# Odd mixer of a hybrid decoder trunk: rotations before the fourth input block, index products and attention units one projection half earlier

## Chip, cores and metric
The kernel runs on one core of a Trainium2 chip. The metric is the device time of one execution in microseconds. The times given are medians of executions of the same program; the profile shows one further execution.

## What is computed
Two decoder layers over 256 tokens of width 1024, all in f32. The change lies in the mixer of the second, odd layer. Cut to that:

```python
def odd_layer(h, ...):
    proj = rms_norm(h, norm_mix) @ w_in                  # 1024 -> 2628 columns
    proj_c, proj_d = split(proj)                         # RWKV-7 | sparse attention
    y_c = rwkv7_time_mix(proj_c, ...)                    # token shift, low-rank gates, 8-head state
    q, k, v, qi, ki, wi = split_cols(proj_d)             # rotate q, k, qi, ki (partial_rope)
    y_d = dsa_attention(q, k, v, qi, ki, wi)
    h = h + concatenate([y_c, y_d]) @ w_out
    return h + moe_swiglu(rms_norm(h, norm_ffn), ...)    # top 2 of 8 experts

def rwkv7_time_mix(p, mu, ...):
    p = p + (prev - p) * mu                              # token shift
    r, k, v, wd, ad, gd = split_cols(p)
    decay, a = gates(tanh(wd) @ w_up), sigmoid(a0 + ad @ a_up)
    # k normalised per head, then a recurrence over the tokens

def dsa_attention(q, k, v, q_idx, k_idx, w_idx):
    score = sum_h relu(q_idx[h] @ k_idx.T) * w_idx[h]    # index products
    sel = top_k(causal(score), 64)
    return softmax(q @ k[sel].T * scale) @ v[sel]        # 8 heads, shared k and v
```

## The kernel before
Every engine has a list of instructions of its own, written out by hand, and works it off in order; semaphores tie the lists together. There is no scheduler: the order in the code is the order on the engine.

The input projection of the odd layer is cut into six blocks of 512 columns (the last narrower) and each block into two halves of the contraction, `odd_half(q, x)`. Blocks 0 to 2 are computed in three split products with `split_half`; blocks 3 to 5 in plain f32 with `whole_half`, 16 products of 128x256 per half. Blocks 0 to 2 bring, in the order of `ODD_PAIRS`, the low-rank inputs (pair 6) and all of the attention's parts (pairs 7 to 10, into `draw`); blocks 3 to 5 bring pairs 0 to 5, the r, k and v of the recurrence. Each pair is copied out of its bank by ScalarE (`odd_copy`, which counts `odd_copied`) and shifted in time by VectorE (`shift`, which counts `shifted`). A copy into the raw buffer waits until the shift but one before it is done.

TensorE puts other work between the halves. The rotations are products with a permutation (the three `C("perm")` matmuls, then the `dup` ones), followed by two pairs of transposes of values and index weights; VectorE finishes the rotation (`rope`). `index_products(t)` makes the index scores of token block t; ScalarE takes the relu (`relu_copy`), VectorE sums the heads (`index_scores`), picks the keys eight at a time (`select_keys`) and makes the mask (`key_mask`). Block 1's 8 rounds of selection are spread, two each, over the first four attention units.

Attention has `UNITS` = 8 units of two heads and one token block; units 0 to 3 are token block 0. It is a pipeline over u: in step u TensorE makes the scores of unit u, the value product of unit u-2 and the transposes of unit u-1, in this order; the transposes wait for `p_ready`. VectorE's `softmax(u)` first normalises unit u-1 (`p_ready`) and then masks the scores of unit u and takes their maximum; ScalarE's `odd_attention(u)` copies the output of unit u-2, takes the exponential of u and copies the transposed weights of u-1.

The RWKV preparation runs in the same loops: `rwkv_step(u - RWKV_LAG)` follows attention step u on VectorE and ScalarE. It needs the gates, which ScalarE makes after `low_rank`, and `low_rank` needs the last projection copy (`odd_copied` 11) and comes behind the last half. Its end is `tilde_done`, behind which the recurrence (the loop over t), the output projection and the experts follow.

Of the kernel before, what the change touches and what calls it, by code (L numbers as in the profile page):

```python
# [145 lines left out]
def trunk(nc, a, consts_dram, out):  # L146
# [297 lines left out]
    UNITS = KM * NT  # L444
# [5 lines left out]
    SCALE = HD ** -0.5  # L450
    RWKV_LAG = 2
    TWO_PI = 6.283185
# [150 lines left out]
    def _(act):  # L603
# [270 lines left out]
        for t in range(NT):  # L874
            act_.activation(Vd[:, t, :], bank[2][:, T * t + HD:T * t + 2 * HD], ACT.Copy)
            act_.activation(wi[:, t, :], bank[2][:, T * t + P + HD:T * t + P + HD + 4], ACT.Copy,
                            scale=4 ** -0.5 * HD ** -0.5).then_inc(sem("kv_copied"), 1)
        odd_copy(5)
        odd_copy(6)
        relu_copy(0)  # L880
        relu_copy(1)
        odd_copy(7)
        odd_copy(8)
        odd_attention(0)
        odd_attention(1)
        odd_copy(9)
        odd_copy(10)
# [29 lines left out]

        for u in range(2, UNITS + 2):
            odd_attention(u)
            rwkv_step(u - RWKV_LAG)  # L920
# [142 lines left out]
    def _(dve):  # L1063
# [381 lines left out]

        shift(0)
        shift(1)
        index_scores(0)
        select_keys(0, TOPK // 8)
        key_mask(0)  # L1450
        index_scores(1)
        shift(2)
        shift(3)

# [43 lines left out]
        for u in range(UNITS + 2):  # L1498
            softmax(u, UNITS, p0, lambda u: md[:, u // KM, :], None)
            if u == 1:  # L1500
                shift(4)
                shift(5)
            if u < KM:
# [335 lines left out]
    def _(pe):  # L1839
# [391 lines left out]
        for q in range(3):  # L2231
            for x in range(2):
                odd_half(q, x)
        pe.wait_ge(sem("odd_copied"), 2)
        odd_half(3, 0)
        pe.wait_ge(sem("odd_copied"), 5)
# [6 lines left out]
        for t in range(NT):  # L2243
            pe_.transpose(bank[2][:, T * t:T * t + P], draw[:, 4, t * P:t * P + P], ident)
            pe_.transpose(bank[2][:, T * t + P:T * t + P + HD + 4], draw[0:HD + 4, 7, t * P:t * P + P],
                          ident[0:HD + 4, 0:HD + 4]).then_inc(sem("kv_T"), 1)
        odd_half(3, 1)

# [26 lines left out]
        pe.wait_ge(sem("odd_rope"), 5)  # L2275
        index_products(0)
        pe.wait_ge(sem("kv_copied"), NT)
        pe.wait_ge(sem("odd_copied"), 4)
        odd_half(4, 0)
        index_products(1)  # L2280
        odd_half(4, 1)
        for u in range(UNITS + 2):
            attention(u, UNITS, lambda f, j: draw[HD * j:HD * j + HD, f, :],
                      lambda f, j: L1["kd"][HD * j:HD * j + HD, :],
                      lambda kt, h: Vd[:, kt, :], L1["pT"], dsa_first)
            if u < 2:
                if u == 0:
                    pe.wait_ge(sem("odd_copied"), 7)
                odd_half(5, u)
                if u:  # L2290
                    low_rank()
# [341 lines left out]
```

## Time and profile before

| | us |
|---|---|
| median of 3 timed runs | 1536.43 |
| lowest and highest | 1536.02, 1536.93 |
| profiled execution, its own time | 1535.13 |
| span of the profiled execution, first to last instruction | 1533.2 |
| TensorE (PE) busy | 1449.2 (95%) |
| VectorE (DVE) busy | 653.6 (43%) |
| ScalarE (ACT) busy | 258.8 (17%) |
| GpSimd (POOL) busy | 30.2 (2%) |
| mean granted clock of TensorE | 0.971 |

The odd mixer is in the page's span from about 385 to 583 us. Times in the trace count from the span's start. PE stands for TensorE, PEld for its weight loads, DVE for VectorE, ACT for ScalarE, SPq for SyncE's load queue. Each f32 product shows as two records, so a half of 16 products reads x32. What stands in brackets is the idle time of the engine ahead of a row and who ended it.

### The profile page before, as it was taken

The page shows a single profiled execution, that of the slowest core. Times are in us where ns is not written, and L with a number is a line of the kernel's source. Part 1 is how long each engine was busy: PE and PEld are TensorE (multiplying, and loading weights), DVE is VectorE, ACT ScalarE, POOL GpSimd, SP SyncE. Part 2 cuts the span into 40 slices and gives each one's busy share as a digit, 9 for nine tenths or more (in the row PEclk, how much of TensorE's full clock was granted, in tenths as well). Part 3 has the DMA queues.
Part 4 walks back from the last instruction along what each step waited for, and adds up shares of the span by engine and source line. Part 5 has one row for each costly group of instructions (what it writes and reads, how often), then busy time and mean ns, then how long its engine had stood idle before and what let it go on. Part 6 is the DMA issues. An engine that isn't in the chain of part 4 may idle for free.

```text
span 1533.2 us, 46200 instructions
## 1 busy us (share of the span) xinstructions
PE 1449.2 (95%) x21517; PEld 1384.2 (90%) x21517; DVE 653.6 (43%) x1549; ACT 258.8 (17%) x441; POOL 30.2 (2%) x33
## 2 busy tenths in 40 slices
PE   7898999998995889999999999999999999999997
PEld 6756899998883778999999999999999999999896
DVE  6942554445567662353334224234224323332327
ACT  2323453434325120200000000000000000000001
POOL 0000000000000210000000000000000000000000
PEclk9998999999995999999999999999999999999998
DMA  9040564445330007699999999999999999999994
GB/s 312 28 165 3 218 220 166 164 162 172 114 110 15 3 3 288 243 387 404 408 396 405 409 382 407 409 382 408 409 379 410 408 380 409 408 385 409 408 373 170
DMA packets 138183, 434.27 MB, mean 283 GB/s; under 512 B 10107, under 2 KB 13285, under 8 KB 137862
## 3 DMA queue, kind: packets, MB, share of 16 engines
q1 hardware_dynamic: 133536, 420.59, 71.2%
q10 hardware_dynamic: 2982, 5.45, 1.0%
q0 software_dynamic: 1472, 5.24, 1.0%
q8 instruction: 171, 2.80, 0.8%
q14 instruction: 22, 0.18, 0.0%
HBM read 426.42 MB, written 4.85 MB: 281 GB/s over the span
## 4 chain that ended last, share of the span: by engine, by line
PE 78%; DMA 9%; DVE 7%; ACT 3%; SPq 2%; issue 1%; ACTq 0%; DVEq 0%
PE bank L2540 31%; PE bank L2538 16%; PE bank L2147 4%; PE bank L2149 4%; PE bank L2148 4%; DMA ring<-in_moe_w_gate 4%; DMA ring<-in_moe_w_down 3%; PE bank L2217 3%; SPq L508 2%; PE bank L1889 2%; PE bank L2120 2%; DMA ring<-in_moe_w_up 2%; PE bank L2135 1%; PE bank L2055 1%; PE bank L2140 1%
## 5 line engine op out<-in xcount | busy, mean ns | idle before, releaser
L2538 PE MATMUL bank<-ring,yT 128*32 128x384 f32 x5760 | 634.4, 491 | 6.2 <-DMA ring<-in_moe_w_gate 5.0
L2540 PE MATMUL bank<-ring,yT 128*32 128x128 f32 x5760 | 635.5, 273 | 0.0
L2540 PEld LDWEIGHTS bank<-ring,yT 128*32 128x32 f32 x5760 | 629.2, 110 | 0.4
L2538 PE MATMUL bank<-ring,arena 128*32 128x384 f32 x2304 | 255.6, 490 | 0.9 <-DMA ring<-in_moe_w_down 0.9
L2540 PE MATMUL bank<-ring,arena 128*32 128x128 f32 x2304 | 255.8, 273 | 0.0
L2540 PEld LDWEIGHTS bank<-ring,arena 128*32 128x32 f32 x2304 | 251.4, 110 | 0.0
L1796 DVE TENSOR_TENSOR arena<-arena,bank 128x384 f32<-128x384 f32 x56 | 28.9, 551 | 426.6 <-PE bank L2540 284.4
L1744 DVE STREAM_TRANSPOSE arena<-arena 32x192 f32<-32x192 f32 x384 | 142.0, 370 | 114.0 <-PE bank L2540 108.9
L2149 PE MATMUL bank<-arena_r,ring_r 128*128 128x256 f32 x608 | 171.9, 283 | 0.0
L2538 PEld LDWEIGHTS bank<-ring,yT 128*32 128x32 f32 x5760 | 163.9, 108 | 7.7 <-issue 4.5
L2147 PE MATMUL bank<-arena_r,ring_r 128*128 128x256 f32 x528 | 148.0, 280 | 1.3 <-DVE arena_r L1324 1.3
L2148 PE MATMUL bank<-arena_r,ring_r 128*128 128x256 f32 x528 | 147.6, 280 | 0.0
L1039 ACT ACTIVATE arena<-bank 128x384 f32<-128x384 f32 x56 | 24.8, 488 | 681.8 <-PE bank L2540 681.8
L1311 DVE TENSOR_TENSOR ring_r<-ring,ring_r 128x2048 fp32r<-128x2048 f32 (+2 forms) x42 | 87.0, 2076 | 86.7 <-ACT ring_r L762 86.5
L2149 PEld LDWEIGHTS bank<-arena_r,ring_r 128*128 128x128 f32 x608 | 115.7, 190 | 0.0
L2147 PEld LDWEIGHTS bank<-arena_r,ring_r 128*128 128x128 f32 x528 | 99.5, 188 | 1.7 <-issue 1.4
L2148 PEld LDWEIGHTS bank<-arena_r,ring_r 128*128 128x128 f32 x528 | 99.1, 188 | 0.1
L762 ACT ACTIVATE ring_r<-ring 128x2048 fp32r<-128x2048 f32 (+2 forms) x42 | 72.9, 1741 | 91.2 <-PE bank L2149 86.4
L2538 PEld LDWEIGHTS bank<-ring,arena 128*32 128x32 f32 x2304 | 63.0, 108 | 1.5 <-DMA ring<-in_moe_w_down 1.5
L1889 PE MATMUL bank<-xnT,ring 128*128 128x256 f32 x192 | 46.8, 405 | 8.0 <-DVE arena L1281 5.7
L1889 PEld LDWEIGHTS bank<-xnT,ring 128*128 128x128 f32 x192 | 38.8, 205 | 15.0 <-DVE arena L1281 5.8
L2217 PE MATMUL bank<-xnT,ring 128*128 128x256 f32 x192 | 42.8, 381 | 0.0
(473 smaller groups left out, 1259.0 us busy)
## 6 DMA issues: line engine op xcount, KB each, us to landing
ring<-in_moe_w_gate SPq DMA_DIRECT2D x56, 2048.0 KB, 23.3
ring<-in_moe_w_up SPq DMA_DIRECT2D x56, 2048.0 KB, 23.3
ring<-in_moe_w_down SPq DMA_DIRECT2D x56, 2048.0 KB, 20.2
ring<-in_ffn_w_gate SPq DMA_DIRECT2D x5, 2048.0 KB, 7.9
ring<-in_ffn_w_up SPq DMA_DIRECT2D x5, 2048.0 KB, 7.8
ring<-in_ffn_w_down SPq DMA_DIRECT2D x5, 2048.0 KB, 7.6
ring<-in_o_w_in SPq DMA_DIRECT2D x5, 2048.0 KB, 7.9
ring<-in_e_w_in SPq DMA_DIRECT2D x4, 2048.0 KB, 16.9
```

The costliest lines, as they stand in the source:

```text
L508: sp.dma_start(w.rearrange("p (k n) -> p k n", k=src.shape[1]), src).then_inc(loaded, 16)
L762: act_.activation(pair(h, src.shape[1])[0], src, ACT.Copy).then_inc(sem("hi_done"), 1)
L1311: v.tensor_tensor(lo, src, hi.bitcast(f32), SUB).then_inc(sem("lo_done"), 1)
L1744: last = v.transpose(to[QUAD[b], :, 32 * a:32 * a + 32], Hc[QUAD[a], 0:to.shape[1], 32 * b:32 * b + 32])
L1889: last = pe_.matmul(dst(i)[0:width, :], w[:, k, i * P:i * P + width], xnT[:, k, :], start=(k == 0), stop=(k == KD - 1))
L2120: last = pe_.matmul(half(bank[2 + i // 2], i), view(n + i // 4)[:, k, (i % 4) * P:(i % 4) * P + P], yT[:, k, :], start=(k == 0), stop=(k = ...
L2147: pe_.matmul(dst, w[0], x[0], start=start, stop=False, skip_group_check=True)
L2148: pe_.matmul(dst, w[1], x[0], start=False, stop=False, skip_group_check=True)
L2149: return pe_.matmul(dst, w[0], x[1], start=False, stop=stop, skip_group_check=True)
L2217: last = pe_.matmul(half(b[i // 2], i), w[:, k, i * P:i * P + P], xnT[:, k, :], start=(k == 0 and i % 2 == 0), stop=(k == KD - 1), skip_gr ...
L2538: pe_.matmul(b[QUAD[m], 0:FM], x(m), w[:, 0:FM], start=start, stop=stop, skip_group_check=True)
L2540: last = pe_.matmul(b[QUAD[3], P * m:P * m + P], x(m), w[:, FM:FB], start=start and m == 0, stop=stop, skip_group_check=True)
```

## The change
No instruction is added or taken away. On TensorE the rotations, with the transposes behind them, move ahead of half (3,0); the index products and the attention steps 0, 1 and 2 each move ahead by one projection half, so that attention step 0 stands before half (4,1), step 1 before (5,0), and step 2 before (5,1), with `low_rank` behind that. On ScalarE the relu copies, and the attention steps 0 to 2, move ahead of copies accordingly. On VectorE the index scores and key selection of block 0 move ahead of shifts 0 and 1, shifts 2 and 3 move from ahead of `softmax(0)` to behind it, and 4 and 5 from behind `softmax(1)` to behind `softmax(2)`. `RWKV_LAG` grows from 2 to 3.

```diff
--- before.py
+++ after.py
@@ -448,7 +448,7 @@
         return (u // NT, u % NT) if base == 0 else (u % KM, u // KM)
 
     SCALE = HD ** -0.5
-    RWKV_LAG = 2
+    RWKV_LAG = 3
     TWO_PI = 6.283185
 
     block = ctx.enter_context(nc.Block())
@@ -875,14 +875,15 @@
             act_.activation(Vd[:, t, :], bank[2][:, T * t + HD:T * t + 2 * HD], ACT.Copy)
             act_.activation(wi[:, t, :], bank[2][:, T * t + P + HD:T * t + P + HD + 4], ACT.Copy,
                             scale=4 ** -0.5 * HD ** -0.5).then_inc(sem("kv_copied"), 1)
+        relu_copy(0)
         odd_copy(5)
         odd_copy(6)
-        relu_copy(0)
         relu_copy(1)
+        odd_attention(0)
         odd_copy(7)
         odd_copy(8)
-        odd_attention(0)
         odd_attention(1)
+        odd_attention(2)
         odd_copy(9)
         odd_copy(10)
 
@@ -915,7 +916,7 @@
                                 L1["st8"][:, 0:16][:, :, None].to_broadcast([P, 16, HD]), ACT.Copy).then_inc(
                     step("kk_wide")[0], 1)
 
-        for u in range(2, UNITS + 2):
+        for u in range(3, UNITS + 2):
             odd_attention(u)
             rwkv_step(u - RWKV_LAG)
         for u in range(UNITS + 2 - RWKV_LAG, UNITS + 2):
@@ -1443,14 +1444,12 @@
             link(v.tensor_scalar(work, work, -2.0e38, NEG, ALU.is_gt, MUL))
             link(v.tensor_tensor(md[:, t, 0:nk], work, C(f"causal{t}")[:, 0:nk], ADD))
 
-        shift(0)
-        shift(1)
         index_scores(0)
         select_keys(0, TOPK // 8)
         key_mask(0)
+        shift(0)
+        shift(1)
         index_scores(1)
-        shift(2)
-        shift(3)
 
         def rwkv_step(u):
 
@@ -1497,9 +1496,9 @@
 
         for u in range(UNITS + 2):
             softmax(u, UNITS, p0, lambda u: md[:, u // KM, :], None)
-            if u == 1:
-                shift(4)
-                shift(5)
+            if u in (0, 2):
+                shift(2 + u)
+                shift(3 + u)
             if u < KM:
                 select_keys(1, TOPK // 8 // KM)
                 if u == KM - 1:
@@ -2231,8 +2230,6 @@
         for q in range(3):
             for x in range(2):
                 odd_half(q, x)
-        pe.wait_ge(sem("odd_copied"), 2)
-        odd_half(3, 0)
         pe.wait_ge(sem("odd_copied"), 5)
         for i, x in enumerate((draw[:, 0:2, :], draw[:, 2:4, :], draw[:, 5:7, :])):
             pe_.matmul(bank[5 + i][:, :], C("perm"), flat(x), start=True, stop=True).then_inc(sem("odd_rope_P"), 1)
@@ -2244,7 +2241,7 @@
             pe_.transpose(bank[2][:, T * t:T * t + P], draw[:, 4, t * P:t * P + P], ident)
             pe_.transpose(bank[2][:, T * t + P:T * t + P + HD + 4], draw[0:HD + 4, 7, t * P:t * P + P],
                           ident[0:HD + 4, 0:HD + 4]).then_inc(sem("kv_T"), 1)
-        odd_half(3, 1)
+        odd_half(3, 0)
 
         def low_rank():
 
@@ -2274,20 +2271,19 @@
 
         pe.wait_ge(sem("odd_rope"), 5)
         index_products(0)
+        odd_half(3, 1)
+        index_products(1)
         pe.wait_ge(sem("kv_copied"), NT)
-        pe.wait_ge(sem("odd_copied"), 4)
         odd_half(4, 0)
-        index_products(1)
-        odd_half(4, 1)
         for u in range(UNITS + 2):
             attention(u, UNITS, lambda f, j: draw[HD * j:HD * j + HD, f, :],
                       lambda f, j: L1["kd"][HD * j:HD * j + HD, :],
                       lambda kt, h: Vd[:, kt, :], L1["pT"], dsa_first)
-            if u < 2:
-                if u == 0:
+            if u < 3:
+                if u == 1:
                     pe.wait_ge(sem("odd_copied"), 7)
-                odd_half(5, u)
-                if u:
+                odd_half(5 if u else 4, u - 1 if u else 1)
+                if u == 2:
                     low_rank()
             u -= RWKV_LAG
             if u == 2:
```

On TensorE, at the rotations. L2149 (now L2148) is the last product of a split half, L2217 (now L2216) a plain half, L2238 to L2245 (now L2235 to L2242) the rotations and transposes. Before, half (3,0) and the first of them:

```order
L2149 MATMUL bank<-arena_r,ring_r 68x256
L2217 MATMUL bank<-xnT,ring 128x256 [waits xn_done,slot4_loaded,odd_copied]
L2217 MATMUL bank<-xnT,ring 128x256 x15
L2238 MATMUL bank<-arena,con 128x512 [waits odd_copied]
L2238 MATMUL bank<-arena,con 128x512 x2
L2241 MATMUL bank<-arena,con 128x256 x4
```

After:

```order
L2148 MATMUL bank<-arena_r,ring_r 68x256
L2235 MATMUL bank<-arena,con 128x512 [waits odd_copied]
L2235 MATMUL bank<-arena,con 128x512 x2
L2238 MATMUL bank<-arena,con 128x256 x4
L2241 MATMUL bank<-con,arena 128x128
L2242 MATMUL bank<-con,arena 128x68
L2241 MATMUL bank<-con,arena 128x128
L2242 MATMUL bank<-con,arena 128x68
L2216 MATMUL bank<-xnT,ring 128x256 [waits xn_done,slot4_loaded]
L2216 MATMUL bank<-xnT,ring 128x256 x15
L2264 MATMUL bank<-arena 128x128 [waits odd_rope]
```

The rotations now follow the split half directly, half (3,0) stands behind them, and the first index products (L2267, now L2264) behind that.

On TensorE, at attention steps 0 and 1. L2024 (now L2023) are the scores of a unit and L2048 (now L2047) its transposes. Before, beginning with the scores of unit 0:

```order
L2024 MATMUL bank<-arena 128x128 [waits relu_done]
L2024 MATMUL bank<-arena 128x128
L2217 MATMUL bank<-xnT,ring 128x256 [waits xn_done,slot6_loaded,odd_copied]
L2217 MATMUL bank<-xnT,ring 128x256 x15
L2024 MATMUL bank<-arena 128x128 [waits sc_read]
L2024 MATMUL bank<-arena 128x128
L2048 MATMUL bank<-con,ring 128x128 [waits p_ready]
L2048 MATMUL bank<-con,ring 128x128
L2217 MATMUL bank<-xnT,ring 128x256 [waits xn_done,slot6_loaded]
L2217 MATMUL bank<-xnT,ring 128x256 x15
L2256 MATMUL bank<-arena 128x256 [waits odd_copied,lora_loaded,lora_in]
```

After, from the same place:

```order
L2023 MATMUL bank<-arena 128x128 [waits relu_done]
L2023 MATMUL bank<-arena 128x128
L2216 MATMUL bank<-xnT,ring 128x256 [waits xn_done,slot5_loaded]
L2216 MATMUL bank<-xnT,ring 128x256 x15
L2023 MATMUL bank<-arena 128x128 [waits sc_read]
L2023 MATMUL bank<-arena 128x128
L2047 MATMUL bank<-con,ring 128x128 [waits p_ready]
L2047 MATMUL bank<-con,ring 128x128
L2216 MATMUL bank<-xnT,ring 128x256 [waits xn_done,slot6_loaded,odd_copied]
L2216 MATMUL bank<-xnT,ring 128x256 x15
L2023 MATMUL bank<-arena 128x128 [waits sc_read]
L2023 MATMUL bank<-arena 128x128
```

Before, halves (5,0) and (5,1) follow the scores of units 0 and 1. Now half (4,1) follows those of unit 0 and half (5,0) those of unit 1 with the transposes of unit 0, and the scores, the value product (L2033) and the transposes of the next step stand ahead of half (5,1).

On VectorE, from the end of `index_scores(1)` to the first key selection of `softmax` step 0. L1390 and L1392 (now L1391 and L1393) are a shift, L1266 to L1270 (now L1267 to L1271) the first part of a unit's softmax, `MAX` (L1436, now L1437) a round of key selection. Before:

```order
L1390 TENSOR_TENSOR arena<-arena 128x512 [waits shifted,odd_copied,dve_chain]
L1392 SCALAR_TENSOR_TENSOR arena<-arena,pcol 128x256 [waits dve_chain]
L1392 SCALAR_TENSOR_TENSOR arena<-arena,pcol 128x256
L1390 TENSOR_TENSOR arena<-arena 128x512 [waits shifted,odd_copied]
L1392 SCALAR_TENSOR_TENSOR arena<-arena,pcol 128x256 [waits dve_chain]
L1392 SCALAR_TENSOR_TENSOR arena<-arena,pcol 128x256
L1266 TENSOR_TENSOR ring<-bank,arena 128x128 [waits sc_done]
L1266 TENSOR_TENSOR ring<-bank,arena 128x128
L1269 TENSOR_REDUCE stat<-ring 128x2 [waits sc_read]
L1270 TENSOR_SCALAR stat<-stat 128x2 [waits dve_chain]
L1436 MAX arena<-arena 128x8
```

After:

```order
L1267 TENSOR_TENSOR ring<-bank,arena 128x128 [waits sc_done,dve_chain]
L1267 TENSOR_TENSOR ring<-bank,arena 128x128
L1270 TENSOR_REDUCE stat<-ring 128x2 [waits sc_read]
L1271 TENSOR_SCALAR stat<-stat 128x2 [waits dve_chain]
L1391 TENSOR_TENSOR arena<-arena 128x512 [waits shifted,odd_copied]
L1393 SCALAR_TENSOR_TENSOR arena<-arena,pcol 128x256 [waits dve_chain]
L1393 SCALAR_TENSOR_TENSOR arena<-arena,pcol 128x256
L1391 TENSOR_TENSOR arena<-arena 128x512 [waits shifted,odd_copied]
L1393 SCALAR_TENSOR_TENSOR arena<-arena,pcol 128x256 [waits dve_chain]
L1393 SCALAR_TENSOR_TENSOR arena<-arena,pcol 128x256
L1437 MAX arena<-arena 128x8
L1438 MATCH_REPLACE arena<-arena 128x256 [waits dve_chain]
```

Shifts 2 and 3 stood ahead of the softmax part of unit 0 and now stand behind it; behind them come, in both, two rounds of selection and then the normalising of unit 0 (L1255 and L1257, now L1256 and L1258).

## Rows read from the trace of the kernel before

**Rows 1.** The page's chain of work that ended last, share of the span by engine.
```profile
...
PE 78%; DMA 9%; DVE 7%; ACT 3%; SPq 2%; issue 1%; ACTq 0%; DVEq 0%
```

**Rows 2.** TensorE's timeline, 407 to 461 us: start, length, line, operation [idle before].
```profile
...
407.75 7.07 PE L2217 MATMUL bank<-xnT,ring 128*128 128x256 f32 x32
414.66 2.74 PE L2238 MATMUL bank<-arena,con 128*128 128x512 f32 x6
...
419.65 7.12 PE L2217 MATMUL bank<-xnT,ring 128*128 128x256 f32 x32
...
442.62 0.49 PE L2024 MATMUL bank<-arena 64*128 64x128 f32 x4
443.04 7.17 PE L2217 MATMUL bank<-xnT,ring 128*128 128x256 f32 x32
450.15 0.49 PE L2024 MATMUL bank<-arena 64*128 64x128 f32 x4
450.57 0.44 PE L2048 MATMUL bank<-con,ring 128*128 128x128 f32 x2
450.84 7.07 PE L2217 MATMUL bank<-xnT,ring 128*128 128x256 f32 x32
458.69 2.29 PE L2256 MATMUL bank<-arena 64*128 64x256 f32 x13 [0.78 <-ACT arena L837]
```

**Rows 3.** VectorE's timeline, 415 to 449 us.
```profile
...
415.72 0.69 DVE L1278 TENSOR_TENSOR ring<-bank,con 128x512 f32<-128x512 f32 x1 [17.17 <-PE bank L2238]
...
443.36 0.69 DVE L1390 TENSOR_TENSOR arena<-arena 128x512 f32<-128x512 f32 x1 [1.79 <-ACT arena L837]
...
444.88 0.48 DVE L1266 TENSOR_TENSOR ring<-bank,arena 128x128 f32<-128x128 f32 x2
...
445.93 0.42 DVE L1436 MAX8 arena<-arena 128x8 f32<-128x256 f32 x1
...
447.89 0.17 DVE L1255 RECIPROCAL stat<-stat 128x2 f32<-128x2 f32 x1
448.09 0.48 DVE L1257 TENSOR_SCALAR ring<-ring,stat 128x128 f32<-128x128 f32 x2
```

**Rows 4.** ScalarE's timeline, 408 to 467 us.
```profile
...
408.23 0.37 ACT L842 ACTIVATE arena<-bank 68x256 f32<-68x256 f32 x1
...
442.73 0.60 ACT L837 ACTIVATE arena<-bank 128x512 f32<-128x512 f32 x1 [2.86 <-PE bank L2217]
...
466.34 0.52 ACT L895 ACTIVATE ring<-bank,pcol 128x256 f32<-128x256 f32 x1
```

**Rows 5.** VectorE's timeline, 471 to 504 us.
```profile
...
471.62 0.16 DVE L1255 RECIPROCAL stat<-stat 128x2 f32<-128x2 f32 x1
...
475.54 0.43 DVE L1444 TENSOR_TENSOR arena<-arena,con 128x256 f32<-128x256 f32 x1
...
484.98 1.23 DVE L1478 TENSOR_TENSOR ring<-arena,ring 128x1024 f32<-128x1024 f32 x1 [2.69 <-ACT ring L908]
...
499.08 1.41 DVE L1490 TENSOR_TENSOR ring<-ring,bank 128x512 f32<-128x512 f32 x2 [0.47 <-PE bank L2306]
...
502.93 1.22 DVE L1495 SCALAR_TENSOR_TENSOR ring<-ring 128x1024 f32<-128x1024 f32 x1
```

**Rows 6.** SyncE's timeline: the load queue.
```profile
...
583.52 1.07 SPq L508 DMA_DIRECT2D ring<-in_moe_w_up  x2
```

**Rows 7.** Stretches: length, busy PE, PEld, DVE, ACT, POOL (count); granted clock, DMA share, GB/s.
```profile
...
78.00:82.60 4.60, 4.60 (x12) 3.68 (x13) 1.62 (x3) 0.00 (x0) 0.00 (x0) 0.52 1.04 398
364.00:368.80 4.80, 0.00 (x0) 0.00 (x0) 4.42 (x8) 2.96 (x7) 0.00 (x0) 0.68 0.49 151
368.90:372.40 3.50, 3.20 (x15) 3.23 (x16) 2.42 (x6) 3.48 (x7) 0.00 (x0) 0.50 0.99 380
386.00:389.00 3.00, 0.00 (x0) 0.00 (x0) 3.00 (x3) 2.65 (x3) 0.00 (x0) 1.00 0.00 0
390.00:393.00 3.00, 3.00 (x16) 3.00 (x16) 3.00 (x4) 0.00 (x0) 0.00 (x0) 0.50 0.21 22
```

## Prediction

> **What bounds the kernel now.** First the page's chain of waits: most of the span is on TensorE, nearly all of that in the expert and dense layers, which the change leaves alone [rows 1]. What the change touches is the odd mixer, and there two stretches must be told apart, so I read the timeline of each engine from 407 us on. In the first stretch TensorE has no gap: from 407.75 us it runs the six plain projection halves (7.1 us each) with the rotations, index products and the score products of attention units 0 and 1 between them, and up to 457.9 us nothing there waits [rows 2]. VectorE and ScalarE work beside it with slack: VectorE sat idle 1.79 us before the fourth-last shift and ScalarE copies each pair as it comes [rows 3, 4]. The second stretch begins when `low_rank` ends (about 461.6 us): ScalarE makes the gates (last at 466.34 us) and from there VectorE and ScalarE lead, until `tilde_done` at 504.1 us [rows 4, 5]; After that the recurrence, the output projection and the experts follow in a chain. Loads for the experts resume only at 583.5 us, released by ScalarE's last mixer copy [rows 6], so they slide with the mixer as well. I therefore take every microsecond on `tilde_done` as a microsecond of the span. The question is how much later or earlier `low_rank` ends, and how much shorter the way from there to `tilde_done` gets.
>
> **First stretch, TensorE.** All products stay, so the order has to be laid out once more with the durations of before.
> (a) The rotations now stand directly behind the last split half and need `odd_copied` at 5, whose fifth step is ScalarE's copy of 408.23 us with 0.37 us. They can start at about 408.7 us, where before a half started at 407.75 us: **+0.9 us** of waiting, which half (3,0) had hidden.
> (b) Rotations, copies and transposes take 5.0 us (414.66 to 419.65 us), wherever they stand: 0. VectorE's chain on them (first at 415.72 us) now begins 6 us earlier and lies beside half (3,0). The first index products need its end; from the first rotation to them is still one half, so they ask as late behind it as before, when they did not wait: 0. ScalarE's first relu goes ahead of two copies, and the second is ready long before the scores of unit 0. 0.
> (c) Half (4,1) ends at 442.62 us before. Now it ends 0.9 us later by (a) and 0.4 us later since the scores of unit 0 (0.42 us from 442.62 to 443.04 us) stand ahead of it: 443.9 us. The scores of unit 1 follow until 444.4 us, and then stand the transposes of unit 0, which need `p_ready`, VectorE's normalised weights.
> (d) When do these come? On VectorE the shifts of pairs 2 and 3 now stand **between** the first half of unit 0's softmax and its second. Shift 3 needs the copy of what half (4,1) has made. Before, it started 0.74 us behind the end of that half (443.36 against 442.62 us) [rows 2, 3]; so now at 444.7 us. Behind it are queued, in order: the shift (443.36 to 444.88, 1.5 us), two rounds of key selection (445.93 to 447.89, 2.0 us), reciprocal and normalising (448.09 plus 0.48, from 447.89: 0.7 us). `p_ready` at 448.9 us. Before, the same chain plus the first softmax part (1.05 us) ended at 448.6 us as well, but TensorE was in half (5,0) until 450.15 us and noticed nothing. Now half (5,0) is queued behind the wait: TensorE stands from 444.4 to 448.9 us, **+4.5 us**. This is the largest term, and it is certain in its kind, since each engine works off its own list in order; a lower bound is 3.5 us if the copy and its signal came 1 us sooner, which nothing suggests.
> (e) Unit 2 (scores 0.42, value product about 0.4, transposes 0.27 us, by the rows of units 0 to 2) moves ahead of half (5,1), and its transposes must wait for ScalarE's copy of the value product (some 0.4 us, by the 0.3 us copy plus signals). Together **+1.5 us** that came behind `low_rank` before. Half (5,1) then begins at 457.8 instead of 450.84 us: `low_rank` is **6.9 us late**. The wait for the last copy (0.78 us) ahead of it stays.
>
> **Second stretch.** What moved out of it: unit 2's softmax (1.7 us on VectorE), and the softmax parts, the last key selection and the mask from 471.62 to 476.0 us (4.4 us), which stood between mixer steps 0 and 1 and now lie beside the making of the gates; step n now comes one unit later in the list. If all of that were on the path it would give 4.4 us. But before, VectorE was not alone on it: it waited 2.69 us for ScalarE's exponentials (484.98 us), and these stand behind the exponential of a unit on ScalarE, now that of the next unit. Laying the lists out from the end of the gates with the durations of before: step 0 and unit 3 by +6.9 us, step 1 +9.3, exponentials of the mixer ready +16.3 (before +18.1), transposed-back factors in VectorE's hands +31 (before 499.08 less 466.85, that is +32.2), and the last 5.1 us to `tilde_done` unchanged. The transposes back stand behind those of unit 7, which eats part again. I take **-1.9 us**, bounds 0 and -4.4 us.
>
> Order alone: 0.9 + 4.5 + 1.5 - 1.9 = **+5.0 us**.
>
> **The clock.** A stall of 4.5 us in front of a dense half has a second price. In this trace TensorE idled 4.8 us (364.0 to 368.8 us) and the mean grant of that stretch was already 0.68; the next 3.5 us of dense products ran at 0.50, that is 1.2 instead of 2.4 GHz. It idled 3.0 us from 386 us, and from 390 to 393 us it was at 0.50. From 78 to 82.6 us 4.6 us of dense work ran at 0.52 [rows 7]. A gap of 0.7 to 1 us, as in (a), shows no such fall. So half (5,0) should start at the lower level and lose half of the 3 to 4.6 us that these stretches lasted: **+2.0 us**, bounds 0 (it doesn't fall) and +3.5 us (all 7.1 us of the half at half rate).
> The Trainium skill, "TensorE: Matmul & The Clock Gate", section "Why this matters for your kernels", says that an idle gap between bursts of products puts the array back to the half clock, and so speaks against any order that opens a gap in dense work. By it the sum is 1543.4 us; by an order that only shifts work without it, 1541.4 us. No row here shows a gap of 3 us or more without the fall, so the trace agrees.
>
> **Sum.** +7.0 us. The profiled execution took 1535.13 us (span 1533.2 and 1.9 us around it), 1.3 us under the median of the three timed runs, 1536.43 us; the difference is added to the median: **1543.4 us**, 0.46% slower.
>
> **Rivals.**
> Stall without the clock's fall. The gap is there but the grant stays at 1.00: +5.0 us, 1541.4 us. For it: whether and when the grant falls depends on where the gap lies. Against: the rows above.
> The stall stays hidden. If the weights of unit 0 came before TensorE asks for them, the sum is 0.9 + 1.5 - 1.9 = +0.5 us, 1536.9 us: no change. For it: the list of work is the same. Against: shift 3 hangs on half (4,1) itself, so the chain of 4.9 us behind that half can't be over 0.5 us after it.
> Faster. One mechanism: the second stretch shortens by more than the first grows. With all of the 4.4 us on the path, and TensorE keeping the higher level into it (its pieces on the path, some 3 us of transposes and value products, halved: 1.5 us), it gives -5.9 us. This beats the first stretch only if the stall of (d) is under 3.5 us and the clock stays up: 1536.43 + 0.9 + 3.0 + 1.5 - 5.9 = 1535.9 us; faster by over 0.2% needs the stall gone as well, 1532.9 us.
> Slower still. Another cold stretch in the recurrence behind `tilde_done`, whose phase against the clock's changes moves: some 2 us on top, 1545.5 us, or a tail that gains nothing, 1545.3 us.
>
> **Chances.** Forecast 0.64, stall without the fall 0.16, slower still 0.08, hidden stall 0.08, faster 0.04. Differences of this kernel below 0.2% (3.1 us) can't be told from no change: slower 0.88, same 0.08, faster 0.04. Range: the low end takes the stall without the fall and 1 us more gain in the tail (1540.4), the high end the forecast with the clock's upper bound and a tail that gains half (1545.9): 1540.3 to 1546.0 us.
>
> **What would show it.** In the changed kernel: rotations at 408.7 us; a TensorE gap of 4 to 5 us ahead of transposes of unit 0 near 449 us, put down to VectorE's L1258; VectorE's shift 3 at 444.7 us, waiting for ScalarE; a granted clock of 0.50 for 3 to 5 us within half (5,0); `low_rank` at about 467.5 us against 458.69 us; the gates' end to `tilde_done` 1 to 3 us shorter; `tilde_done` near 511 us. I would be wrong if that gap were under 2 us, or if the time behind `tilde_done` did not simply slide.

## The result and the profile after

| | before | after |
|---|---|---|
| first comparison, median (runs) | 1536.68 us (4) | 1546.61 us (4, 1543.84 to 1548.67) |
| second comparison, median (runs) | 1536.12 us (17) | 1544.33 us (6, 1541.61 to 1547.92) |
| profiled execution, span | 1535.13, 1533.2 us | 1543.84, 1542.0 us |
| mean granted clock | 0.971 | 0.968 |

The changed kernel is slower: ratio 1.0067, 95% interval 1.0055 to 1.0080 (+9.9 us in the medians), and in the second comparison 1.0057, 1.0041 to 1.0073 (+8.2 us). I had forecast 1543.4 us, with 1546.0 us as the high end. The direction holds; the size does not: the first median lies 3.2 us above the forecast and 0.6 us above the high end.

TensorE's timeline of the changed kernel, in the stretch of [rows 2]:

```profile
406.04 0.28 PE L2148 MATMUL bank<-arena_r,ring_r 128*68 128x256 f32 x1
407.06 2.84 PE L2235 MATMUL bank<-arena,con 128*128 128x512 f32 x6 [0.74 <-ACT arena L842]
...
435.54 7.17 PE L2216 MATMUL bank<-xnT,ring 128*128 128x256 f32 x32
442.65 0.49 PE L2023 MATMUL bank<-arena 64*128 64x128 f32 x4
447.61 0.69 PE L2047 MATMUL bank<-con,ring 128*128 128x128 f32 x2 [4.47 <-DVE ring L1258]
448.09 9.62 PE L2216 MATMUL bank<-xnT,ring 128*128 128x256 f32 x32
...
458.97 0.41 PE L2047 MATMUL bank<-con,ring 128*128 128x128 f32 x2 [0.47 <-ACT yT L688]
...
467.07 1.10 PE L2253 MATMUL bank<-arena 64*128 64x256 f32 x4 [0.78 <-ACT arena L837]
```

There are four things to see. The rotations wait 0.74 us for ScalarE. TensorE stands for 4.47 us ahead of the transposes of unit 0, and VectorE's normalising (L1258) ends the wait. Half (5,0) behind it takes 9.62 us where all others take 7.1 us. `low_rank` starts at 467.07 us, 8.4 us later than in [rows 2], although this execution's last split product started 1.6 us earlier.

VectorE's timeline shows what TensorE waited for:

```profile
443.38 0.69 DVE L1391 TENSOR_TENSOR arena<-arena 128x512 f32<-128x512 f32 x1 [1.84 <-ACT arena L837]
444.11 0.88 DVE L1393 SCALAR_TENSOR_TENSOR arena<-arena,pcol 128x256 f32<-128x256 f32 x2
444.91 0.42 DVE L1437 MAX8 arena<-arena 128x8 f32<-128x256 f32 x1
...
446.87 0.17 DVE L1256 RECIPROCAL stat<-stat 128x2 f32<-128x2 f32 x1
447.07 0.48 DVE L1258 TENSOR_SCALAR ring<-ring,stat 128x128 f32<-128x128 f32 x2
```

The shift waits for ScalarE's copy of half (4,1); then come the rest of the shift, two rounds of selection and the normalising: 4.2 us of queue from 443.38 to the release of TensorE.

The granted clock (third number from the right) in half (5,0) and in what follows the mixer, from windows over the changed kernel:

```profile
448.00:457.70 9.70, 9.70 (x36) 7.77 (x34) 2.96 (x11) 1.15 (x5) 0.00 (x0) 0.73 0.17 69
449.00:450.00 1.00, 1.00 (x4) 0.81 (x3) 0.93 (x4) 0.79 (x5) 0.00 (x0) 0.50 0.59 234
...
510.80:517.70 6.90, 6.23 (x114) 5.50 (x114) 5.47 (x14) 2.49 (x5) 3.94 (x5) 0.75 0.01 4
590.00:594.00 4.00, 4.00 (x11) 3.29 (x12) 0.00 (x0) 0.00 (x0) 0.00 (x0) 0.60 0.83 196
```

The first products of the recurrence in the changed kernel, and VectorE's instructions ahead of them:

```profile
505.68 1.41 DVE L1489 TENSOR_TENSOR ring<-ring,bank 128x512 f32<-128x512 f32 x2 [4.12 <-PE bank L2302]
...
509.52 1.22 DVE L1494 SCALAR_TENSOR_TENSOR ring<-ring 128x1024 f32<-128x1024 f32 x1
...
510.80 0.45 PE L2330 MATMUL bank<-ring 64*64 64x128 f32 x8 [2.02 <-DVE ring L1494]
...
513.01 1.87 PE L2338 MATMUL bank<-ring,arena 64*64 64x128 f32 x32
...
519.55 0.28 PE L2376 MATMUL bank<-ring 64*64 64x64 f32 x4
```

The same products in the kernel before:

```profile
504.20 0.45 PE L2334 MATMUL bank<-ring 64*64 64x128 f32 x8 [0.61 <-DVE ring L1495]
...
505.59 1.06 PE L2342 MATMUL bank<-ring,arena 64*64 64x128 f32 x32
...
511.88 0.28 PE L2380 MATMUL bank<-ring 64*64 64x64 f32 x4
```

Before, TensorE idled 0.61 us here and ran the products of L2342 in 1.06 us; now it idles 2.02 us and the same products (L2338) take 1.87 us. The first 5.2 us of before, at a clock of 1.00, have become 6.9 us. Part of that is regained: the first product of L2376 (L2380 before) stands 8.75 us behind the start instead of 7.68 us, so the slow start costs 1.1 us. By the start of the second token block (35.5 against 34.4 us) the loss is still 1.1 us. VectorE, for its part, waits 4.12 us for the transposes back (L2302), where it waited 0.47 us before [rows 5]; they ran at the lower level and took 1.92 us.

Where the 8.8 us between the two spans lie (lengths, us; e5 is the unaltered kernel before, profiled once more, and e1 the changed one):

| stretch | before | e5 | after | e1 |
|---|---|---|---|---|
| start to the last split product | 407.6 | 406.3 | 406.0 | 406.4 |
| to `low_rank` | 51.1 | 51.0 | 61.1 | 60.5 |
| to the last gate's start | 7.6 | 7.7 | 7.6 | 7.6 |
| to the first recurrence product | 37.9 | 37.8 | 36.1 | 36.1 |
| to the output projection | 78.9 | 79.1 | 79.2 | 80.1 |
| to the expert products | 45.3 | 50.0 | 48.2 | 46.7 |
| to the end | 904.8 | 905.0 | 903.8 | 904.4 |

The mixer up to the first recurrence product accounts for +8.2 us in this pair (+7.6 for e1). The +2.9 us ahead of the experts can't be put down to the change: the same kernel before took 45.3 us there in one execution and 50.0 us in another.

### The profile page after: what moved, and what is told of

Same layout as the page of the kernel before. It is cut to its first block, busy times and chain, and to the rows that moved or that the text cites. A ratio compares the mean times of both kernels' runs of the same rounds, so it can differ in the third digit from the quotient of the medians.

```text
span 1542.0 us, 46201 instructions
## 1 busy us (share of the span) xinstructions
PE 1455.0 (94%) x21517; PEld 1388.1 (90%) x21517; DVE 653.6 (42%) x1549; ACT 259.2 (17%) x441; POOL 30.6 (2%) x33
## 4 chain that ended last, share of the span: by engine, by line
PE 84%; DVE 8%; DMA 4%; ACT 2%; SPq 1%; issue 1%; ACTq 0%; DVEq 0%
PE bank L2536 34%; PE bank L2534 18%; PE bank L2146 4%; PE bank L2148 4%; PE bank L2147 4%; DMA ring<-in_moe_w_gate 4%; PE bank L2216 3%; PE bank L2119 2%; PE bank L1888 1%; PE bank L2134 1%; PE bank L2054 1%; PE bank L2139 1%; SPq L508 1%; DVE xnT L1084 1%; PE bank L2378 1%
## 5 line engine op out<-in xcount | busy, mean ns | idle before, releaser
L2148 PE MATMUL bank<-arena_r,ring_r 128*128 128x256 f32 x608 | 171.7, 282 | 0.0
L2148 PEld LDWEIGHTS bank<-arena_r,ring_r 128*128 128x128 f32 x608 | 115.5, 190 | 0.0
L2216 PE MATMUL bank<-xnT,ring 128*128 128x256 f32 x192 | 45.3, 397 | 0.0
```

The lines of the kernel that those rows point to most:

```text
L2148: return pe_.matmul(dst, w[0], x[1], start=False, stop=stop, skip_group_check=True)
L2216: last = pe_.matmul(half(b[i // 2], i), w[:, k, i * P:i * P + P], xnT[:, k, :], start=(k == 0 and i % 2 == 0), stop=(k == KD - 1), skip_gr ...
```

## The experiments

Spare products (`keep_warm`) are 128x256 products into an unused bank. Nothing of the computation is left out in any run. Ratios are against the kernel before on the same chip.

**e1, the changed kernel once more.**

> The changed kernel once more, with nothing altered, for a second profile and more times beside the kernels below. Theory (the stall of about 4.5 us ahead of half (5,0), the clock's fall on it, and cold stretches behind the mixer whose place varies): median 1544 to 1548 us; the way from the last split half to the first recurrence product reproduces within 1 us (+8 us against before), and the spread between executions sits behind it. Rival (the spread sits in the mixer itself): low_rank's place against the last split half differs by over 2 us between the two profiles.

1544.33 us, ratio 1.0057 (1.0041 to 1.0073). The stall is 4.47 us again and half (5,0) takes 9.07 us. So stall and low clock belong to the order of the lists; how much of the half is lost varies (1.95 and 2.5 us).

**e2, the changed kernel without the shift ahead of the selection.**

```diff
-            if u in (0, 2):
-                shift(2 + u)
-                shift(3 + u)
+            if u in (1, 2):
+                shift(2 * u)
+                shift(2 * u + 1)
```

> Only VectorE's shifts 2 and 3 move, from behind softmax step 0 to behind step 1, so that the weights of unit 0 are normalised before half (4,1) ends. Theory (the stall is the whole difference, by itself and by the clock that falls on it): no TensorE gap ahead of the transposes of unit 0, half (5,0) in 7.1 us at a granted clock of 1.00, and about -7 us against the changed kernel on the first recurrence product: 1536 to 1539 us, no difference from before that can be told (order alone +0.5 us). Rival (the earlier rotations and the longer lag cost by themselves): it stays 4 us or more above before.

1538.46 us (12 runs), ratio 1.0014 (1.0004 to 1.0024), 5.9 us less than e1. TensorE's timeline of e2:

```profile
442.80 0.49 PE L2023 MATMUL bank<-arena 64*128 64x128 f32 x4
443.23 0.44 PE L2047 MATMUL bank<-con,ring 128*128 128x128 f32 x2
443.50 7.07 PE L2216 MATMUL bank<-xnT,ring 128*128 128x256 f32 x32
...
503.64 0.70 PE L2330 MATMUL bank<-ring 64*64 64x128 f32 x8 [2.31 <-DVE ring L1494]
```

The transposes follow the scores without a gap and the half runs at full rate. Placing two shifts one step later on VectorE removes stall and clock loss, 5.9 of 8.2 us. The +2.3 us that is left was forecast at +0.5 us (the sum without the stall). In its profile, 0.8 us of it is in the mixer, and the recurrence takes 80.1 us against 78.9 us; its first product of L2376 stands 9.02 us behind the start instead of 7.68 us, so 1.3 us are lost at the slow start.

**e3, one dose less: selection of unit 0 moved behind the next normalising.**

```diff
-            if u < KM:
-                select_keys(1, TOPK // 8 // KM)
+            if 0 < u < KM:
+                select_keys(1, TOPK // 8 // KM * (2 if u == 1 else 1))
```

> The first two rounds of key selection (2.0 us on VectorE) move from ahead of the normalising of unit 0 to behind softmax step 1. Theory: the gap ahead of the transposes shrinks by 2.0 us, from 4.5 to 2.5 us, so low_rank comes at least 2.0 us earlier; if so short a gap no longer lets the clock fall, another 2.5 us (half (5,0) 7.1 instead of 9.6 us): -2 to -4.5 us against the changed kernel. Rival (something else than the chain shift, selection, normalising ends the gap): the gap stays at 4.5 us.

1541.98 us, ratio 1.0036 (1.0022 to 1.0050). TensorE's timeline, then windows of e3:

```profile
445.78 0.44 PE L2047 MATMUL bank<-con,ring 128*128 128x128 f32 x2 [2.50 <-DVE ring L1258]
446.05 8.76 PE L2216 MATMUL bank<-xnT,ring 128*128 128x256 f32 x32
```
```profile
447.00:448.00 1.00, 1.00 (x4) 0.81 (x3) 0.93 (x4) 0.95 (x5) 0.00 (x0) 0.50 1.03 426
450.00:451.00 1.00, 1.00 (x7) 0.87 (x6) 0.90 (x5) 0.00 (x0) 0.00 (x0) 1.00 0.06 16
```

Two rounds of selection taken out of the queue shorten the gap by 1.97 us, as the term of 2.0 us in (d) says, and the median is 2.35 us below that of e1. The half is still slow (8.76 us): 2.5 us of idle time was followed by the same fall of the clock as 4.47 us.

**e4, the changed kernel with the gap filled.**

```diff
+                if base and u == 1:
+                    keep_warm(bank[4], 9)
                 pe.wait_ge(sem("p_ready"), base + w + 1)
```

> TensorE runs 9 spare products (keep_warm on bank 4, some 4.0 us) in the gap of 4.5 us ahead of the transposes of unit 0; everything else is the changed kernel. Theory (the stall has a second price through the clock): the transposes come at the same time, within 0.2 us, half (5,0) takes 7.1 instead of 9.6 us, the granted clock stays at 1.00 there, and low_rank comes 2.5 us earlier; on the median -2.5 us. Rival (the clock's fall costs nothing in the end, since VectorE or ScalarE lead): low_rank earlier, but the first recurrence product not.

TensorE's timeline of e4:

```profile
444.50 4.15 PE L1860 MATMUL bank<-con 128*128 128x256 f32 x18
449.04 0.44 PE L2049 MATMUL bank<-con,ring 128*128 128x128 f32 x2 [0.39 <-DVE ring L1258]
449.31 7.07 PE L2218 MATMUL bank<-xnT,ring 128*128 128x256 f32 x32
```

1542.98 us, ratio 1.0046 (1.0032 to 1.0060). The transposes come as late behind the scores as without the spare products, 4.97 us, but the half takes 7.07 us. The wait and the clock are therefore two prices: from the split products to the first recurrence product e4 takes 102.0 us, e1 104.2 and the first changed one 104.8 us. In the medians only 1.35 us of these 2.2 to 2.8 us shows, where 2.5 us was expected, and the intervals of e1 and e4 overlap: the second price is shown by the profiles, not by the times.

**e7, the shift moved, in the kernel before.** Here shifts 2 and 3 stand behind `softmax(0)` too, but TensorE's order is that of before.

```diff
         index_scores(1)
-        shift(2)
-        shift(3)
...
-            if u == 1:
-                shift(4)
-                shift(5)
+            if u < 2:
+                shift(2 * u + 2)
+                shift(2 * u + 3)
```

> One part alone on the kernel before: VectorE's shifts 2 and 3 stand behind softmax step 0 instead of ahead of it; TensorE and ScalarE as before. Theory (the stall needs both parts, for here half (5,0), 7.1 us long, stands between the end of half (4,1) and the transposes): the weights of unit 0 are ready near 449 us and TensorE asks at 450.6 us: no gap, no difference (0 +- 0.5 us on low_rank). Rival (VectorE's new order costs by itself): a gap ahead of the transposes, low_rank over 1 us later.

1536.69 us (12 runs), ratio 0.9997 (0.9986 to 1.0009), and no gap:

```profile
450.41 0.49 PE L2022 MATMUL bank<-arena 64*128 64x128 f32 x4
450.83 0.44 PE L2046 MATMUL bank<-con,ring 128*128 128x128 f32 x2
```

The same edit costs about 6 us with the changed order on TensorE and nothing without it. The stall needs both parts.

**e10, only the lag.**

```diff
-    RWKV_LAG = 2
+    RWKV_LAG = 3
```

> RWKV_LAG = 3 alone on the kernel before. Theory (the longer lag pays only since unit 2 has moved ahead of low_rank; alone it puts unit 3's softmax, whose scores wait for ScalarE's output copy behind the gates, ahead of mixer step 0): low_rank as before, first work of step 0 about 7 us later than before (473.6 instead of 467 us), first recurrence product some 4 to 5 us later: 1540 to 1542 us. Rival (the lag shortens the way from the gates to tilde_done by itself, by the 1.8 us seen in the changed kernel): 1534.5 us.

1541.77 us, ratio 1.0031 (1.0019 to 1.0043). VectorE's timeline of e10:

```profile
466.39 0.48 DVE L1266 TENSOR_TENSOR ring<-bank,arena 128x128 f32<-128x128 f32 x2
...
469.73 0.43 DVE L1444 TENSOR_TENSOR arena<-arena,con 128x256 f32<-128x256 f32 x1
470.19 1.14 DVE L1460 TENSOR_SCALAR ring<-arena,pcol 128x256 f32<-128x256 f32 x4
```

The gates' last instruction started at 462.82 us, and before step 0 of the mixer (L1460) started 0.62 us behind it (466.96 us behind 466.34 us, [rows 4]). Here it came at 470.19 us, 7.4 us behind it, behind a unit's softmax, two rounds of selection and the mask. From gates to recurrence it is 42.8 us against 37.9 us. So the later lag costs 5 us by itself. The changed kernel, with the later lag and the attention steps moved up together, is 1.8 us shorter there; no run has the moved steps with a lag of 2, so what each gives in it is not shown.

e10 also shows idle time that the clock did not answer. Ahead of the recurrence TensorE idles 2.51 us, longer than in e1 (2.29 us), and the products behind it take 0.45 and 0.40 us, as in the kernel before. And the gap at 386 us of [rows 7], which all kernels here have in common, is followed by a granted clock of 1.00 in e10:

```profile
387.21 0.36 PE L2147 MATMUL bank<-yT_r,ring_r 128*128 128x256 f32 x1 [3.41 <-DVE arena_r L1324]
```
```profile
388.00:391.00 3.00, 3.00 (x28) 3.00 (x27) 3.00 (x3) 0.00 (x0) 0.00 (x0) 1.00 0.17 18
```

**e6 and e9, only the rotations moved** (the same kernel, run twice).

```diff
-        pe.wait_ge(sem("odd_copied"), 2)
-        odd_half(3, 0)
         pe.wait_ge(sem("odd_copied"), 5)
...
+        odd_half(3, 0)
         odd_half(3, 1)
```

> One part alone on the kernel before: the rotations and the transposes behind them stand ahead of half (3,0), all else as before. Theory: TensorE waits 0.7 to 0.9 us for ScalarE's last copy ahead of the rotations, everything behind comes 0.7 to 0.9 us later: +0.8 us, not told from before by its times. Rival (the earlier rotations give something, since VectorE gets its work sooner): low_rank no later than before against the last split half.

> The rotations alone ahead of half (3,0), a second time, since its times fell into two groups (1534 to 1539 and 1542 to 1543 us) round a profile that shows +0.8 us in the mixer. Theory (the part costs 0.8 us; the slower group is chance in where lower-clock stretches fall outside the mixer): a median of 1536 to 1539 us. Rival (the earlier rotations cost 4 to 5 us in most executions by something the first profile missed): the median is near 1542 us again, and a profile of a slow execution shows where.

e6: 1541.88 us (10 runs), 1.0028 (1.0016 to 1.0040). e9: 1539.44 us (12 runs), 1.0015 (0.9999 to 1.0030). The rotations wait 0.74 us and `low_rank` comes 1.0 and 0.9 us later behind the split products, which is term (a). But in the times both miss what was expected: by its ratio e6 is 4.3 us slower than before (2.5 to 6.1), not 0.8 us, e9 2.3 us (-0.2 to 4.6), and the runs of this one program spread from 1532.5 to 1543.7 us. Windows from 486 us to behind the first recurrence products, of e6 and then of e9:

```profile
486.00:501.70 15.70, 11.83 (x70) 7.79 (x66) 11.77 (x26) 9.95 (x24) 0.01 (x1) 0.61 0.00 1
501.70:507.00 5.30, 4.70 (x116) 3.98 (x118) 4.21 (x12) 2.58 (x6) 4.02 (x5) 1.00 0.02 3
```
```profile
486.00:505.90 19.90, 15.63 (x71) 10.34 (x72) 13.87 (x32) 10.02 (x24) 2.04 (x4) 0.50 0.00 1
505.90:511.00 5.10, 4.42 (x107) 4.01 (x107) 3.34 (x11) 1.84 (x4) 0.98 (x2) 0.84 0.01 3
```

In e6 the clock came back before the recurrence, in e9 it stayed at 0.50 up to it: gates to recurrence 38.0 and 40.0 us. The end of that stretch in e9:

```profile
502.55 1.22 DVE L1495 SCALAR_TENSOR_TENSOR ring<-ring 128x1024 f32<-128x1024 f32 x1
...
503.03 2.93 PE L1861 MATMUL bank<-con 128*128 128x256 f32 x6
505.89 0.71 PE L2333 MATMUL bank<-ring 64*64 64x128 f32 x8
```

VectorE was done at 503.77 us, and TensorE began the recurrence only at 505.89 us: at the lower level its last attention products and the three spare products ahead of the wait, 2.93 us here and 1.56 us in e6, had become the longer way. The profiled execution of e9 took 5.5 us more than that of e6: 2.0 us of it here, 1.7 us ahead of the experts, and 2.2 us in what comes before the last split product, where no kernel differs. Whether most executions of this order lose those 2 us, and why six of e6's ten runs lie together at 1541.9 to 1542.7 us, is not settled by two profiles. So the cost of the moved rotations beyond the wait stays open.

**e11, the tail kept busy.** The kernel before, with spare products ahead of the transposes of steps 2 to 5:

```diff
+                if base and u in (2, 3, 4, 5):
+                    keep_warm(bank[4], {2: 10, 3: 3, 4: 7, 5: 3}[u])
```

> The kernel before with spare products on bank 4 in TensorE's idle time of attention steps 2 to 5 (10, 3, 7 and 3 of them), so that the clock stays at the upper level behind low_rank. Theory (VectorE and ScalarE lead there, TensorE's pieces on the path are few): granted clock near 1.00 from 462 to 500 us, gates to first recurrence product shorter by 0.5 to 1 us only. Rival (the lower clock in that stretch is what makes it 38 us long): shorter by 3 us or more, 1533 us.

1537.55 us (12 runs), ratio 1.0002 (0.9990 to 1.0013). Windows of e11:

```profile
467.50:486.00 18.50, 13.34 (x73) 9.40 (x72) 14.81 (x40) 9.72 (x25) 0.00 (x0) 0.93 0.00 1
486.00:505.40 19.40, 12.89 (x72) 8.31 (x70) 15.32 (x34) 10.27 (x26) 0.00 (x0) 0.71 0.00 0
```

The clock rose to 0.93 in the first part, where before it was 0.50, and from gates to recurrence it still took 37.9 us. So in this part VectorE and ScalarE lead, not TensorE's clock, as the prediction read it. The last part was not tested: there the clock had fallen again (the transposes back took 1.92 us), and e9 shows that at its end the lower level costs 2 us. Nor does e11 say anything of the changed kernel, where VectorE waits 4.12 us for those transposes.

**e8 and e12, more spare products ahead of the recurrence**, in e2 and in the changed kernel:

```diff
-WARM = {"norm_in": [0, 5, 5, 5], "norm_out": [8, 0, 0, 10], "tilde": 3, "group_norm": 8,
+WARM = {"norm_in": [0, 5, 5, 5], "norm_out": [8, 0, 0, 10], "tilde": 6, "group_norm": 8,
```

> The kernel without the stall (shifts 2 and 3 behind softmax step 1) and 6 instead of 3 spare products ahead of the wait for tilde_done, which fill the 2 us in which TensorE idles there. Theory (that idle time lets the clock fall on the first recurrence products): granted clock 1.00 there, recurrence start to output projection 78.9 instead of 80.1 us; first product no more than 0.3 us later; -1.2 us against the kernel without the stall, so 1536.5 to 1538 us beside 1536. Rival (the fall has nothing to do with that gap): the stretch stays cold at 0.5 for 3 us and the way stays at 80.1 us.

> The changed kernel with 6 instead of 3 spare products ahead of the wait for tilde_done. Theory (the cold stretch at the first recurrence products comes from the 2 us of idle time ahead of tilde_done): granted clock 1.00 at the first recurrence products, their block 5.2 instead of 6.9 us, -1 to -1.5 us on the way from the recurrence's start to the output projection; median 1542.5 to 1544.5 us. Rival: the stretch stays.

e8: 1538.40 us (12 runs), ratio 1.0014 (1.0003 to 1.0025); e12: 1546.65 us (6 runs), ratio 1.0060 (1.0045 to 1.0075). TensorE's timeline of e12:

```profile
508.15 3.35 PE L1860 MATMUL bank<-con 128*128 128x256 f32 x12
512.32 0.45 PE L2330 MATMUL bank<-ring 64*64 64x128 f32 x8 [0.82 <-DVE ring L1494]
...
512.70 0.40 PE L2330 MATMUL bank<-ring 64*64 64x128 f32 x8
```

The products of L2330 take 0.40 us again, where e2's took 0.65 us, and the recurrence takes 79.2 us in e8 and 79.1 us in e12 against 80.1 us in e2 and e1. Up to the first product of L2376 it takes 7.7 us in both, as in all eight profiles that start at the upper level, against 8.74 to 9.02 us in after and e1 to e4: the spare products bring back 1.1 to 1.3 us. The whole stretch is a worse measure, since the clock falls again in its middle at places that differ: from the start of the second token block on it takes 43.4 us (e10) to 45.5 us (e6), and e6, which starts at the upper level, takes 79.9 us in all. Yet the ratios to the kernel before did not move (1.0014 in e2 too, 1.0057 in e1), and both medians lie above what was expected. A microsecond is less than these comparisons can tell, so the slow start of the recurrence is seen in profiles and its share in the times stays unproven.

**e5, the kernel before, once more.**

> The kernel before, unaltered, for a second profile. Theory (the four profiles with the change share a cold stretch at the first recurrence products, since TensorE idles some 2 us ahead of tilde_done there, and it is no accident of one execution): here the granted clock is 1.00 at the first recurrence products, as in the first profile of before; recurrence start to output projection within 0.5 us of the 78.9 us of the first profile. Rival (where the lower clock falls behind the mixer differs by chance only): a cold stretch at the recurrence's start here too. The way from the output projection to the experts (45.3 us before, 46.7 to 48.2 us in the four others) may fall anywhere in 45 to 48 us; if it is over 46.5 us here, that difference was chance.

1537.17 us (12 runs), ratio 1.0004 (0.9994 to 1.0014), against 33 runs from 1532.5 to 1539.5 us. Windows of e5 where the output projection begins, then of the kernel before at the same place:

```profile
581.90:586.00 4.10, 4.10 (x12) 3.32 (x13) 0.00 (x0) 0.00 (x0) 0.00 (x0) 0.60 0.74 198
```
```profile
583.10:586.00 2.90, 2.90 (x13) 2.57 (x14) 0.00 (x0) 0.00 (x0) 0.00 (x0) 1.00 0.75 143
```

One program, two executions: in one the output projection starts at the lower level, in the other not. The changed kernel's profile has it too (0.60 from 590 to 594 us, above), and e1, the same kernel, spends 1.5 us less there.

## Why the prediction was right in direction and too small

**(a) Rotations, +0.9 us.** Right for the wait: it is 0.74 us, and e6 and e9 put `low_rank` 1.0 and 0.9 us later. But the times of e6 put this part at +4.3 us (2.5 to 6.1), and what there is beyond the wait the term has not; e9's profile shows one place for it, 2.0 us at the end of the tail.

**(b) No cost from the moved rotation chain.** Right: nothing waits at the index products, and the halves follow each other without a gap up to 442.6 us.

**(c), (d) The stall, +4.5 us.** Right in place, cause and size: 4.47 us in both profiles, put down to L1258. e3 took the two selection rounds out and 1.97 us went, e2 took the shift out and all of it went, e7 shows that the shift alone, without the new TensorE order, costs nothing that can be told (-2.2 to +1.4 us).

**(e) Unit 2 ahead of half (5,1), +1.5 us.** Right: from the end of half (5,0) at 457.64 us to half (5,1) at 459.21 us it is 1.57 us.

**The clock, +2.0 us.** Right: +2.5 and +1.95 us. e4 shows that it is a price apart from the wait. The Trainium skill, "TensorE: Matmul & The Clock Gate", section "Why this matters for your kernels", says that an idle gap between bursts puts the array back to half the clock. The runs agree: with a gap the half takes 8.76 to 9.62 us (e3, e1, after), without one 7.07 us (e2, e4). But not every gap does it: behind the 3.41 us gap of e10 the clock stayed at 1.00, where [rows 7] show 0.50 behind the same gap. The prediction had the fall from rows of one execution.

**The second stretch, -1.9 us.** Right: 36.1 instead of 37.9 us in both profiles, -1.8 us. The rival that the whole 4.4 us lay on the path fell. That TensorE's clock does not hold the tail back is shown for its first part alone (e11).

**Mixer in total.** Predicted +7.0 us, measured +8.2 and +7.6 us from the last split product to the first recurrence product. The terms above, as measured, add up to +7.6 and +7.1 us (0.9 + 4.47 + 1.57 + 2.5 or 1.95 - 1.8). The transposes behind the stall ran at the lower clock, another 0.2 us (0.48 us to the half instead of 0.27); the last 0.3 to 0.4 us are not assigned.

**The step that failed** is the one that closes the first part: "I therefore take every microsecond on `tilde_done` as a microsecond of the span." With it went a weight of 0.08 for another stretch at the lower level, and a high end built from the bounds of single costs. Three things were wrong in it.
First, the recurrence did not just slide. In all of after, e1, e2, e3 and e4 TensorE idles 2.0 to 2.3 us ahead of `tilde_done`, where it idled 0.61 us before, and from the first or second group of products on it runs at 1.2 GHz for some 3 us. That costs 1.1 us (after, e4) to 1.3 us (e1, e2, e3) up to the first product of L2376. I had priced this at 2 us and given it a small chance; it is there in every one of these profiles. The whole stretch, 80.1 us in e1, e2 and e3 and 79.2 and 79.1 us in after and e4 against 78.9 and 79.1 us before, shows it less clearly, since later falls of the clock move it by 2 us. e2, which has no stall at all, is still 2.3 us (0.6 to 3.7) slower than before where 0.5 us was forecast, and its profile has 0.8 us of it in the mixer and 1.3 us at the start of the recurrence. In the times this share stays likely and not shown: e8 and e12 took the slow start away without moving the ratio, and e2 also has the moved rotations, whose cost in the times of e6 is not explained. Why the clock falls there is not settled either: with less idle time (e8 1.77 us, e12 0.82 us) it did not fall, but with 2.51 us in e10 it did not fall either.
Second, where the clock falls behind the mixer differs from execution to execution: 45.3 and 50.0 us ahead of the experts in two profiles of the kernel before. Three timed runs within 0.9 us had looked like a kernel that repeats itself; 33 runs span 7 us. A range for a median of four such runs has to be wider than the mechanism alone asks for.
Third, the sum of the two. All ten times of the changed kernel have their middle at 1545.1 us, 1.7 us above the forecast and inside the range; the first four of them alone have it at 1546.6 us. So of the miss of 3.2 us about half is a cost that I left out or undersized (0.6 to 1.2 us in the mixer, 1.1 to 1.3 us at the recurrence's start) and about half the scatter of four runs. This split is an estimate from these medians.

Of the rivals, the stall without the clock's fall, the hidden stall and the faster kernel are refuted by the rows of half (5,0) and L2047. Slower still (1545.5 us) was the nearest to the measured time. The cold stretch that it names is there, at 1.1 to 1.3 us instead of 2 us.

No version here beats the kernel before. The nearest with any of the change in it is e7, which only moves shifts and is no different.

## What to carry to other kernels

When work is moved up on one engine, ask for each wait in it what is queued ahead of the releasing instruction on its own engine; a harmless-looking swap (two shifts, e7) becomes a stall of 4.5 us once the waiter comes one projection half sooner (e1), and moving the two shifts out of the way gave more than filling the gap (5.9 us in e2 against 1.35 us in e4). Try a pipeline lag together with the order that it is meant for: lag 3 alone cost 5 us, and with the moved steps the same stretch was 1.8 us shorter. And measure how far one program's own executions spread before a range of a few microseconds is drawn around a forecast.

## What was not expected of the hardware

Idle time of 2.5 us ahead of a dense half was followed by a clock of 0.50 for some 3 us, with a loss of 1.7 us (e3); I had rows only for gaps of 3.0 us and more. The answer to the same gap is not the same each time: behind 3.4 us of idle time at 386 us the clock fell in the kernel before and not in e6 and e10. The unaltered kernel differs by 7.4 us between executions (1532.9 to 1540.3 us in the 23 runs beside e9), and where two of its profiles differ by 4.7 us in one stretch, one of them shows the lower clock at the start of it. Up to the last split product all profiled kernels run the same code, and took from 404.0 us (e6) to 409.2 us (e8). One order (e6, e9) reached both 1532.5 and 1543.7 us, a spread wider than the cost of the change under study. A TensorE at the lower level can become the engine that others wait for where it was not before: in e9 it kept the recurrence waiting 2.1 us behind VectorE's last instruction.
